# Cached keys of four streams turned by VectorE in the first projection, and the recurrent heads' sums at another place

## What is computed

```python
def fox_sample(x, cache_k, cache_v, cache_lf, w_in, b_f, w_out):      # 8 streams, 256 cached rows, 16 heads of 64
    q, k, v, lf = fox_project(x, w_in, b_f)
    k_all = jnp.concatenate([cache_k, k], axis=1)
    v_all = jnp.concatenate([cache_v, v], axis=1)
    c = jnp.cumsum(jnp.concatenate([cache_lf, lf], axis=1), axis=1)
    o = fox_attend(q, k_all, v_all, c[:, P:], c, kpos[P:], kpos)      # softmax(q k' / 8 + c_q - c_k), masked
    return o.reshape(B, T, D_MODEL) @ w_out, k, v, lf

def hgrn_chunk_step(S, inp):                                          # 8 heads of 128
    b = jnp.cumsum(g, axis=1)
    decay = jnp.exp(jnp.where(causal, b[:, :, None] - b[:, None, :], -jnp.inf))
    scores = jnp.einsum('bthc,bshc,btshc->bhts', q, k, decay)
    ...
```

## Time and profile before

| | |
|---|---|
| time, median of 3 runs | 1865.68 us (1864.34 to 1867.13) |
| the profiled execution: time, span | 1866.66 us, 1864.9 us |
| granted TensorE clock, mean | 0.998 of full speed |
| busy: PE, DVE, ACT, POOL | 99%, 54%, 38%, 13% |
| HBM read, written | 251.58 MB, 21.57 MB |
| first projection | about 10 to 123.5 us |
| first attention loop | 123.5 to about 200 us |
| recurrent layer's slots | about 535 to 765 us |
| fourth layer's attention loop | 1478.3 to about 1550 us |

### The profile page before, as it was taken

The page is one execution under the profiler, slowest core; times in us unless marked ns, Lnnn a source line. Parts: engine busy times, 40 slices in busy tenths (PEclk is TensorE's granted clock), DMA queues, the critical chain, the costliest instruction groups (busy, mean ns, idle before and its releaser), DMA issues.

```text
span 1864.9 us, 28909 instructions
## 1 busy us (share of the span) xinstructions
PE 1837.5 (99%) x11886; PEld 1629.1 (87%) x11886; DVE 1002.5 (54%) x1602; ACT 709.5 (38%) x1144; POOL 246.1 (13%) x397
## 2 busy tenths in 40 slices
PE   9999999999999999999999999999999999999998
PEld 8777799998888887799998899998797768999986
DVE  4557654343567768744443565455564566444334
ACT  4246343333255454333332253233242463433321
POOL 3114070000011223230000100101111230000000
PEclk9999999999999999999999999999999999999999
DMA  7456344433353433444433445656654573444432
GB/s 239 143 180 233 115 149 128 131 125 125 113 167 110 127 104 107 122 139 125 130 130 125 151 121 174 206 184 202 204 163 145 175 268 125 147 124 128 133 124 79
DMA packets 190050, 276.14 MB, mean 148 GB/s; under 512 B 15357, under 2 KB 131181, under 8 KB 189920
## 3 DMA queue, kind: packets, MB, share of 16 engines
q1 hardware_dynamic: 169632, 205.57, 34.6%
q0 software_dynamic: 20288, 68.74, 11.6%
HBM read 251.58 MB, written 21.57 MB: 146 GB/s over the span
## 4 chain that ended last, share of the span: by engine, by line
PE 87%; DVE 6%; ACT 3%; DMA 2%; issue 1%; POOL 0%; SPq 0%; DVEq 0%; ACTq 0%
PE ps L1710 15%; PE ps L1712 15%; PE ps L1711 15%; PE ps L1722 9%; PE ps L1720 9%; PE ps L1721 9%; PE ps L2082 1%; DVE w_lo L831 1%; PE ps L2049 1%; ACT w_hi L480 1%; DVE stats L882 1%; PE ps L2069 1%; PE ps L1743 1%; PE ps L1948 1%; PE ps L2008 1%
## 5 line engine op out<-in xcount | busy, mean ns | idle before, releaser
L831 DVE TENSOR_TENSOR w_lo<-w_raw,w_hi 128x1024 fp32r<-128x1024 f32 x370 | 450.5, 1228 | 663.2 <-ACT w_hi L480 662.2
L480 ACT ACTIVATE w_hi<-w_raw 128x1024 fp32r<-128x1024 f32 x370 | 388.9, 1059 | 802.0 <-DMA w_raw<-in_w_ffn_in_dram 354.9
L1710 PE MATMUL ps<-xT_hi,w_hi 128*128 128x384 f32 x1568 | 528.4, 337 | 3.3 <-DVE xT_lo L849 1.9
L1712 PE MATMUL ps<-xT_hi,w_lo 128*128 128x384 f32 x1568 | 526.9, 336 | 0.0
L1711 PE MATMUL ps<-xT_lo,w_hi 128*128 128x384 f32 x1568 | 526.9, 336 | 0.0
L1710 PEld LDWEIGHTS ps<-xT_hi,w_hi 128*128 128x128 f32 x1568 | 294.8, 188 | 6.2 <-issue 3.3
L1711 PEld LDWEIGHTS ps<-xT_lo,w_hi 128*128 128x128 f32 x1568 | 294.8, 188 | 0.1
L1712 PEld LDWEIGHTS ps<-xT_hi,w_lo 128*128 128x128 f32 x1568 | 294.8, 188 | 0.0
L1722 PE MATMUL ps<-w_hi,hT_lo 128*128 128x512 f32 x528 | 210.6, 399 | 0.0
L1721 PE MATMUL ps<-w_lo,hT_hi 128*128 128x512 f32 x528 | 208.1, 394 | 0.0
L1720 PE MATMUL ps<-w_hi,hT_hi 128*128 128x512 f32 x528 | 207.6, 393 | 0.2 <-DVE w_lo L831 0.2
(11 more groups left out here) (338 smaller groups left out, 2000.2 us busy)
## 6 DMA issues: line engine op xcount, KB each, us to landing
w_raw<-in_w_ffn_in_dram SPq DMA_DIRECT2D x352, 256.0 KB, 3.2
w_raw<-in_w_ffn_out_dram SPq DMA_DIRECT2D x176, 256.0 KB, 2.9
w_raw<-in_w_fox_in_dram SPq DMA_DIRECT2D x96, 256.0 KB, 3.0
v_c<-in_cache_fox_v_dram POOLq DMA_DIRECT2D x32, 512.0 KB, 4.9
w_raw<-in_w_hgrn_in_dram SPq DMA_DIRECT2D x64, 256.0 KB, 3.0
k_c<-in_cache_fox_k_dram POOLq DMA_DIRECT2D x16, 512.0 KB, 5.1
w_raw<-in_w_fox_out_dram SPq DMA_DIRECT2D x32, 256.0 KB, 3.0
k_nat<-in_cache_fox_k_dram POOLq DMA_DIRECT2D x8, 1024.0 KB, 10.4
```

The source lines that it names most:

```text
L480: nc.scalar.activation(w_hi[:, slot, :], w_raw[:, slot, :], ACT.Copy).then_inc(hi_ready, 1)
L831: V.tensor_tensor(w_lo[:, slot, :], w_raw[:, slot, :], w_hi[:, slot, :].bitcast(F32), ALU.subtract).then_inc(lo_ready, 1)
L1710: mm(out, w_hi[:, slot, cols], x_hi[:, k, :], start=k == 0, stop=False, skip_group_check=True)
L1712: last = mm(out, w_lo[:, slot, cols], x_hi[:, k, :], start=False, stop=k == KD - 1, skip_group_check=True)
```

## The change

**Keys.** The cached keys of the first layer's last four streams (units 8 to 15) are no longer turned by TensorE in the loop. GpSimd loads them in four pieces of 1 MB (`k_nat_f`) during the first projection, VectorE turns one piece after each of its steps 4, 8, 11 and 14, and GpSimd stores them to a new tensor `keys_f` in HBM. SP loads the turned units in the loop, between the sixth and the seventh unit of the output projection's weights. Units 8 to 15 then take the paths of the fourth layer: keys from `k_t`, the new frames' keys added by GpSimd, ScalarE's copy of the turned probabilities in two pieces, another PSUM bank for the output.

GpSimd's order in the first layer changes with it: the first piece is loaded where two loads of `k_c` and two of `v_c` were; the laying of constants then follows without waiting for unit 6; the first three loads of `k_c` come behind the fourth piece's stores; the first three of `v_c` come behind the store of the new keys, once the pieces have landed in HBM and `c_lo` is done.

**Sums.** For heads 1 to 6 of the recurrence `sums(ha, 0)` stands between the direct and the small packed products of head `ha - 1`, and VectorE's `gT_lo` (now `low_logs`) ahead of its `low_sides`. Head 7 keeps the old order, and so does head 0.

```diff
@@ constants
+NAT = 8
+TURN_MIX = {4: 0, 8: 1, 11: 2, 14: 3}
@@ buffers
+        k_nat_f = sb("k_nat_f", [P, TWIN, TCOLS], after("rcp"))
+        k_turn_f = sb("k_turn_f", [P, TCOLS // 32, 32, TWIN], after("k_t"))
...
+        def come_turned(i, n):
+
+            return i == AHEAD or n >= NAT
@@ SyncE
+            def turned_later_keys():
+
+                f = FOX[0]
+                for n in range(NAT, 2 * DB):
+                    b, hf = n // 2 - DB // 2, n % 2
+                    if n == NAT:
+                        sync.wait_ge(*at(KEYS_F["stored"], 64 * 4))
+                    sync.wait_ge(*at(f["s_scores"], n - KV + 1))
+                    if n == NAT + 1:
+                        sync.wait_ge(*at(f["ktr"], NAT))
+                    sync.dma_start(k_t[:, n % KV, :, 0:PAST], keys_f[b, hf * WCOLS:(hf + 1) * WCOLS, :].rearrange(
+                        "(g p) k -> p g k", p=P)).then_inc(KEYS_F[f"in{n % KV}"][0], 16)
...
-                        chunks(w_fox_out[j], s["out"], 2)
+                        chunks(w_fox_out[j], s["out"], 2, 0, RING)
+                        turned_later_keys()
+                        chunks(w_fox_out[j], s["out"], 2, RING)
@@ ScalarE, attention loop
-                    if 1 <= n < HEADS and i != AHEAD:
+                    if 1 <= n < HEADS and not come_turned(i, n):
                         act.wait_ge(*at(f["ktr"], n + 1))
@@ VectorE
+            def turn_later_keys(n):
+
+                dve.wait_ge(*at(KEYS_F["loaded"], 16 * (n + 1)))
+                if n:
+                    dve.wait_ge(*at(KEYS_F["stored"], 64 * n))
+                for a in range(TWIN):
+                    ins = V.transpose(k_turn_f[:, :, :, a], k_nat_f[:, a, :])
+                ins.then_inc(KEYS_F["turned"][0], 1)
@@ VectorE, projection, last in step u
+                    if not i and u in TURN_MIX:
+                        turn_later_keys(TURN_MIX[u])
@@ VectorE, attention loop
-                        if n and i != AHEAD:
+                        if n and not come_turned(i, n):
                             key_sides(n, KT_BANKS + 1)
@@ VectorE, recurrence
+                    if ka == 0 and ha < HG - 1:
+                        low_logs(ha)
                     if kb == 0:
                         low_sides(hb)
+                    if ka == 0 and ha == HG - 1:
+                        low_logs(ha)
@@ GpSimd, first layer
+                else:
+                    pool.wait_ge(unit_used, m0 + 1)
+                    load_later_keys(0)
                     load_gb(0)
...
-                    pool.wait_ge(unit_used, m0 + 12)
-                    load_k(KV - 1)
-                load_v(KV - 1)
+                    for n in range(1, 4):
+                        store_later_keys(n - 1)
+                        load_later_keys(n)
+                    store_later_keys(3)
+                    for n in range(KV):
+                        load_k(n)
...
                 store(0, f["kstored"], fox_k_prompt, fox_k_sample)
+                if i != AHEAD:
+                    pool.wait_ge(*at(KEYS_F["stored"], 64 * 4))
+                    pool.wait_ge(*at(f["c_lo"], 3))
+                    for n in range(KV):
+                        load_v(n)
@@ TensorE, attention loop
-                    if 2 <= n < HEADS and i != AHEAD:
+                    if 2 <= n < HEADS and not come_turned(i, n):
                         s_keys(n, KT_BANKS)
@@ TensorE, recurrence
                     if kb == 1:
                         pairs(hb)
+                        if ha and ha < HG - 1:
+                            sums(ha, 0)
+                        pairs_packed(hb)
...
-                    if ka and (ha or ka == 2):
+                    if ka and (ha and (ka > 1 or ha == HG - 1) or ka == 2):
                         sums(ha, 2 * ka - 2)
```

More of the change, by code:

```diff
@@ L124, in trunk_program @@
         keys_t = nc.dram_tensor("keys_t", [DB, D, PAST], F32)
+        keys_f = nc.dram_tensor("keys_f", [DB // 2, D, PAST], F32)
         base = -(-nc.sbuf_base // 64) * 64
@@ L182, in trunk_program @@
         ktc = sb("ktc", [P, 4, PAST + DT], after("v_c"))
+        k_nat_f = sb("k_nat_f", [P, TWIN, TCOLS], after("rcp"))
+        k_turn_f = sb("k_turn_f", [P, TCOLS // 32, 32, TWIN], after("k_t"))
+        assert after("k_nat_f") <= after("k_t") and after("k_turn_f") <= after("v_c")
         x_s = sb("x_s", [P, 2, P], after("ktc"))
@@ L304, in trunk_program @@
             "stored": 16 * 4})))
-        HGR = {i: {k: (sem(f"hgrn_{k}"), 0) for k in (
+        TAKEN = {"st0_in": 16 * 4, "st1_in": 64 * 4, "snew": 4, "gate": 2 * DB - NAT}
+        HGR = {i: {k: (sem(f"hgrn_{k}"), TAKEN.get(k, 0)) for k in (
             "consts", "pconst", "masks", "pmask", "ng_in", "q_ev", "f_ev", "t01_ev", "t2_ev", "sig", "sgg", "gate",
@@ L316, in trunk_program @@
         H = HGR[KINDS.index("hgrn")]
-        KEYS = {"loaded": (H["st0_in"][0], 16 * (HG // 2)), "stored": (H["st1_in"][0], 16 * (HG // 2)),
-                "turned": (H["snew"][0], 2 * HG), "new": (H["gate"][0], 2 * GRP),
-                "in0": (x_in[1], 16), "in1": (x_in[2], 16), "in2": (turned_in, 0)}
+        KEYS_F = {"loaded": (H["st0_in"][0], 0), "stored": (H["st1_in"][0], 0), "turned": (H["snew"][0], 0),
+                  "new": (H["gate"][0], 0), "in0": (x_in[1], 16), "in1": (x_in[2], 16), "in2": (turned_in, 0)}
+        KEYS = {"loaded": at(H["st0_in"], 16 * (HG // 2)), "stored": at(H["st1_in"], 16 * (HG // 2)),
+                "turned": at(H["snew"], 2 * HG), "new": at(H["gate"], 2 * GRP),
+                **{f"in{c}": at(KEYS_F[f"in{c}"], 16 * len([n for n in range(NAT, 2 * DB) if n % KV == c])) for c in range(KV)}}
+        def come_turned(i, n):
+            return i == AHEAD or n >= NAT
         CT_AFTER, CT_BANK, CT_LF = (8, 9, 10, 11, 12), (3, 7, 3, 7, 3), 4
@@ L326, in out_bank @@
         def out_bank(i, n):
-            return KT_BANKS if i == AHEAD and n < HEADS - 1 else SPT_BANK
+            return KT_BANKS if come_turned(i, n) and n < HEADS - 1 else SPT_BANK
         block = ctx.enter_context(nc.Block())
@@ L1419, in new_keys @@
                     now = slice(SEQ + DT * (n // 2), SEQ + DT * (n // 2) + DT)
-                    G.tensor_copy(k_t[:, n % KV, :, PAST:], kT[:, 4 * (n % 2):4 * (n % 2) + 4, now]).then_inc(KEYS["new"][0], 1)
+                    G.tensor_copy(k_t[:, n % KV, :, PAST:], kT[:, 4 * (n % 2):4 * (n % 2) + 4, now]).then_inc(
+                        KEYS["new"][0], 1)
                 def store(n, marked, kp, ks):
@@ L2062, in s_pairs @@
                         pe.wait_ge(*at(KEYS["new"], n + 1))
+                    elif n >= NAT:
+                        pe.wait_ge(*at(KEYS_F[f"in{n % KV}"], 16 * ((n - NAT) // KV + 1)))
+                        pe.wait_ge(*at(KEYS_F["new"], n - NAT + 1))
                     else:
@@ L2067, in s_pairs @@
                         rows, k = slice(32 * g, 32 * g + 32), 4 * (n % 2) + g
-                        keys = k_t[:, n % KV, g, :] if i == AHEAD else ktc[:, g, :]
+                        keys = k_t[:, n % KV, g, :] if come_turned(i, n) else ktc[:, g, :]
                         last = mm(ps[rows, SS_BANK, 0:PAST + DT], qs[:, k, n // 2, :, :].rearrange("p e q -> p (e q)"), keys,
```

39 lines of the change are left out of this document (26 added, 13 removed).

## The result

The changed kernel takes 1868.34 us (median of 22 runs, 1864.74 to 1872.24), the kernel before 1865.17 us (22 runs on the same chip, 1863.47 to 1868.13). The ratio is 1.0017, 95% interval 1.0012 to 1.0023: slower by 3.2 us, where I had forecast 3.4 us faster. The time also lies above the top of my range, 1867.6.

What follows compares the result with a forecast made beforehand. TensorE was taken to bound the kernel, busy 1837.5 of 1864.9 us. Attention loop -6.4, projection +4.5 and recurrent heads -1.5 summed to -3.4 us, so 1862.3 us, with an 8-in-10 range of 1858.8 to 1867.6.

Steps and rivals of the forecast that it cites:

- have room: First projection, VectorE behind the second transpose block: a low part and the next eviction run late without holding TensorE; no cost.
- is covered: First projection, other engines: GpSimd's k_c and value loads, the key store and VectorE's c_lo still come in time; no cost.
- Attention loop: First layer's attention loop: units 8 to 15 lose their key transposes, four pairs at 1.60 us each, -6.4 us on TensorE.
- Recurrent heads: Recurrent stage, small products: moved sums fill 0.5 us of each of three waits for low_sides, -1.5 us (bounds 0 and -2.8).
- First stall and clock: First projection, near 82 us: TensorE waits 2.8 us for lf_tok behind block 2; the clock drop then costs 1.7 us.
- Second stall: First projection, turn_keys(4): block 3 delays the new keys' copy by 0.7 us more, which falls away after the clock drop.
- Block 0 free: First projection: the first transpose block starts at about 40 us, ends at 44.4, next load there by 57.5; no cost.
- Block 1: First projection: second transpose block, 62.1 to 66.4 us; next eviction done near 68.2, TensorE wanting it half a microsecond later.
- Rival 4: Projection's 1 MB key loads so slow that the kernel is slower by over 0.2%: at 14 us, +4.9, 1870.6 us; chance 0.06.
- Rival 3: Projection's key loads land in 12.6 us: 8.3 us of stalls, one clock drop, net +2.1, 1867.8 us; chance 0.14.
- Rivals 2 to 4: L is a projection key load's landing time; the first of these: within 7.4 us, no stall, -7.9, 1857.8 us; chance 0.10.
- rival 1: First projection: the stalls come but the clock holds, 3.5 in place of 4.5, so -4.4, 1861.3 us; chance 0.17.
- rival 5: Attention loop: turned keys land late and half the 6.4 us is lost, -0.2, 1865.5 us; chance 0.03.

Runs made afterwards that it cites:

- e1: The kernel before with only the recurrent heads' edit (sums and low_logs moved): 1862.60 us, ratio 0.9986.
- e10: The kernel before with only w_hi and w_lo of the first projection asked for one step later, as a control: 1865.49 us, ratio 1.0005.
- e5: The changed kernel with the third and fourth transpose blocks moved to after VectorE's steps 12 and 15, behind the copies TensorE waits for: 1870.67 us, ratio 1.0024.
- e12: e11 with load_gb issued late, in the first attention loop, as in e6: 1863.57 us, ratio 0.9991.
- e8: The changed kernel with all transfers and blocks kept, but the first projection's w_hi and w_lo asked for one step later: 1861.29 us, ratio 0.9980.
- e6: The changed kernel with load_gb issued in the first attention loop, not right behind the first 1 MB load of keys: 1866.31 us, ratio 1.0009.
- e11: e8 with the last transpose block after VectorE's step 15, behind the copy of the new keys: 1860.18 us, ratio 0.9980.
- e7: The changed kernel with e5's block places, load_gb late as in e6, and two of three k_c loads issued later: 1866.99 us, ratio 1.0009.
- e3: The changed kernel without VectorE's transpose blocks, all transfers kept (cached keys of four streams wrong): 1867.80 us, ratio 1.0007.

## Why the prediction was wrong

The step that failed is the one on what the other engines carry beside TensorE: that small things behind block 1 "have room" and that what is queued behind on the other engines "is covered". It stood in the sum at nothing and cost 5.5 us, through weights of SP that landed late. Term by term:

- **Attention loop, -6.4**: right. The three distances that could be read are 7.96, 7.77 and 7.70 against 9.30, 6.1 in all with the fourth pair. The loads of `k_t` were in time.
- **Recurrent heads, -1.5**: right in mechanism (1.4 us left in three waits); alone it measured -2.5, with the forecast inside its interval. Beside the keys' part there is something more: a wait of 1.2 us at L2283 (at 731.80) for which the profile names no releaser. It is 0.3 in the kernel before and absent in e1 and e10, and every version with the keys' part has 0.7 to 2.6 us of it. Its cause is open.
- **First stall and clock, 2.8 + 1.7**: in the trace just so, with the landing of 10.2 us that I took (issued at 72.39, block 2 at 82.63), only 3 us later than drawn, at 85.2 to 88.0. That VectorE and TensorE were late by the same 3.2 us is luck. And my reason was not the only one. In this trace the block is the later of two causes: from the 84.9 of its `w_hi` the late weights alone would have left about 1.1 us (an estimate from these rows). e5, with the block moved away, has 1.8; e12 has the full 2.8 from the block with the weights' order mended. Two causes lay on the same copy, and taking away the one that I knew of left most of the wait.
- **Second stall, falls away**: right for the changed kernel. When e8 took the first away, it came, with 2.2 us and 1.7 of clock.
- **Block 0 free**: TensorE doesn't wait for it, but it is not free. It begins at 44.42 and not at about 40, since the weights issued from 22 to 30 us, beside the first 1 MB load and `load_gb`, land in 8.3 us (5.5 in the kernel before), and VectorE stands 11.73 us for them. So load 1 goes out at 51.37 in place of about 47, where it slows the weights whose `w_hi` comes at 61.74. In e6, without `load_gb` there, the block begins at 40.45, load 1 at 47.40, and the waits at L1998 are gone.
- **Block 1, "whose users have room"**: wrong. I had written that TensorE wants the next eviction only half a microsecond after it is done, and called that room. VectorE came to the block 3.5 us later than I had it (65.61 in place of 62.1), since the `w_lo` ahead was late, and TensorE stood 2.0 us for the eviction ahead of the block and 0.9 for the one behind. In e8, with the block in place at 60.47, neither wait is there.
- **"What is queued behind on the other engines is covered"**: wrong, and the larger part of the error with the point above. I checked when GpSimd's own loads of `k_c` would be in time, and they were (issued at 104.92, used without a wait). I did not ask what those transfers do to somebody else's. SP's stream of weights stood in my sum only as something that slows the new loads, never the other way round. I had put that at nothing without a reason. Cost: 2.6 us at `kT`, and the lateness behind the 2.9 at L1998: together the 5.5 us that the sum lacks.

In the sum: forecast -6.4 + 4.5 - 1.5 = -3.4; the traces give -6.1 + 10.0 and the recurrent part -1.5 to -2.5, so +1.4 to +2.4, and up to 0.9 more with the new wait at L2283. The profiled execution is 1.8 us over the median of the kernel before, the median of all runs 3.2; what the others have beyond it no trace shows. Rival 4 had the right sign by a mechanism that did not happen: it wanted loads over 13.4 us, and they landed in 8.7 to 10.2. Rival 3 had nearly the right number, +2.1, by loads of 12.6 us that did not come either. None of my rivals was the real one. Rivals 2 to 4 varied L, one number, rival 1 the clock behind the same stall, rival 5 the loads in the loop: the blocks and my own loads were all that I followed. The sign that I had named for being wrong, TensorE waiting at another place of the projection, came.

The price stood in the trace of before, beside the very rows from which I took L. The first line is of SP's loads issued from 1137 to 1139 us, while the second 1 MB load goes out, the second is the `w_hi` of ScalarE that waited for them:
```profile
w_raw<-in_w_ffn_in_dram SPq DMA_DIRECT2D x2, 256.0 KB, 8.9
...
1148.45 1.06 ACT L480 ACTIVATE w_hi<-w_raw 128x1024 fp32r<-128x1024 f32 x1 [9.07 <-DMA w_raw<-in_w_ffn_in_dram]
```
The load issued just ahead of them, from 1135 to 1138 us, landed in 3.6 us. TensorE did not wait there, so nothing called attention to it.

A page points the same way: the Trainium skill, page "DMA: Bandwidth & Descriptors", section "Queues, rings and completion order", says that each DMA engine takes turns between the queues that have work for it. The trace agrees as far as it can show it: SP's loads go on beside GpSimd's, at 5.5 and 8.0 us in place of 3.4 and 2.9.

## What to carry to other kernels

When a change adds bulk transfers, price them first at the loads that are there already: take the median landing of the existing stream, ask what it becomes when it shares the DMA engines (best where the trace of before already has such a transfer: 3.6 and 8.9 us here), and then follow the first engine that waits for that stream in order, with everything small that is queued behind that wait. An eviction that stands behind "prepare the weights of six units on" has as its deadline the landing of those weights, however small it is; asking for them one step later was worth 6.5 us here and nothing where the loads were quick. And a wait may have two sufficient causes: a forecast that hits its size has not shown its reason until each cause has been taken away alone.

## What the runs showed of the hardware that I had not expected

- The 256 KB loads of SP land in 2.9 to 3.4 us in these stretches of the kernel before, in 5.5 with 1 MB loads and 256 KB stores of GpSimd beside them, and in 8.0 in the burst where the DMA engines are busy throughout (from 110 to 120 us of the changed kernel their share is 1.00, at 369 GB/s). The slowdown is not in proportion to the engines' busy share: before, the share was 0.65 from 70 to 80 us with 3.4 us of landing, after it is 0.84 with 5.5.
- The clock after waits of like size: 2.8 us (`lf_tok`) and 2.2 us (e8) were each followed by 1.7 us of lost clock, while 2.6 us (`kT`, changed kernel) and 2.0 us (e11) were followed by a granted clock of 1.00. Two waits of 2.0 us differ (0.83 from 85 to 95 us in e7, behind the wait for `lf_tok`, against 1.00 in e11), and so do two of 2.4 for `kT` (0.84 from 110 to 120 us in e5, 1.00 in e6). Between 2.0 and 2.8 us the length of a single wait does not tell whether the clock falls.
- Some of these kernels spread more from run to run: 7.5 us over the changed kernel's 22 runs and 9.3 over e3's 11, against 4.7 over 22 of before, 2.7 over e1's 11 and 3.6 over e8's 11. That landing times which differ from run to run decide the waits would explain it, but each kernel has one trace, and it is not shown.
